# A two-block transformer kernel: four modulation chunks moved from TensorE to VectorE, one low part issued earlier, two orders on TensorE changed

## The reference, cut to what matters

```
# block 1, twice:
hn = rms_norm(x, ln1);  proj = hn @ w_in
y  = concat[ 6 MoBA heads, 4 mLSTM heads (normed, gated), 6 sliding-window heads with a sink ]
x  = x + y @ w_out
x  = x + square(relu(rms_norm(x, ln2) @ w_up)) @ w_down
# block 2, twice (with a second stream ctx of 256 tokens that shares weights):
mod   = silu(c) @ w_mod[l] + b_mod[l]          # 1024 -> 6*1024
mod_c = silu(c_ctx) @ w_mod[l] + b_mod[l]      # the same weights, for ctx
sh1, sc1, gt1, sh2, sc2, gt2 = split(mod, 6)
z = (rms_norm(x, g1) * (1 + sc1) + sh1) @ w_in_2   # attention over [x ; ctx], conv, Fourier
x = x + gt1 * merge(z);   x = x + gt2 * mlp(modulate(x, g2, sh2, sc2))
```

## Time and profile before

| | |
|---|---|
| median of 3 runs | 1736.59 us (1736.1 to 1736.89) |
| the profiled execution, its own time | 1736.67 us |
| its span in the trace | 1734.8 us |
| granted TensorE clock, mean over the span | 0.999 |
| RAW transfers of w_mod (1024 KB each) | 28 |
| WM transfers of w_mod (512 KB each) | 40 |
| DMA traffic | 343.67 MB, mean 198 GB/s |

### The profile page before, as it was taken

How to read it: one execution, slowest core, us unless ns; L and a number is a source line. 1 busy time by engine, 2 the same in 40 slices (tenths; PEclk the granted TensorE clock), 3 DMA queues, 4 the chain that set the end, 5 groups by cost and what they waited for, 6 DMA issues and landing times.

```text
span 1734.8 us, 23892 instructions
## 1 busy us (share of the span) xinstructions
PE 1715.5 (99%) x9753; PEld 1443.1 (83%) x9753; DVE 1246.3 (72%) x1518; ACT 930.4 (54%) x1238; POOL 46.7 (3%) x36
## 2 busy tenths in 40 slices
PE   8999999999999999999999999999999999999999
PEld 7868888886888898788888898778888887888887
DVE  6986888598687765577777857677666666775665
ACT  6555554556544554555555546546455546564453
POOL 0200000011000000000000000000000000000000
PEclk9999999999999999999999999999999999999999
DMA  8476776756777655455776554357555754345552
GB/s 297 157 245 204 243 243 209 264 157 219 257 239 238 203 190 173 146 174 190 265 236 226 183 170 168 112 192 244 196 193 194 235 176 147 134 146 194 194 194 73
DMA packets 226837, 343.67 MB, mean 198 GB/s; under 512 B 8109, under 2 KB 117033, under 8 KB 226729
## 3 DMA queue, kind: packets, MB, share of 16 engines
q1 hardware_dynamic: 225896, 340.87, 58.7%
q10 hardware_dynamic: 832, 1.28, 0.2%
HBM read 341.07 MB, written 1.06 MB: 197 GB/s over the span
## 4 chain that ended last, share of the span: by engine, by line
PE 90%; DVE 5%; ACT 1%; SPq 1%; issue 1%; DMA 1%; POOL 0%; POOLq 0%; ACTq 0%; DVEq 0%
PE PS L2263 15%; PE PS L2265 15%; PE PS L2264 15%; PE PS L2319 15%; PE PS L2323 8%; PE PS L2308 2%; PE PS L2309 2%; PE PS L2310 2%; PE PS L2706 1%; PE PS L2708 1%; PE PS L2707 1%; PE PS L2799 1%; PE PS L2787 1%; PE PS L2776 1%; PE PS L2726 1%
## 5 line engine op out<-in xcount | busy, mean ns | idle before, releaser
L1363 DVE TENSOR_TENSOR LO<-RAW,HI 128x2048 fp32r<-128x2048 f32 x271 | 618.6, 2290 | 263.7 <-ACT HI L795 262.9
L795 ACT CAST HI<-RAW 128x2048 fp32r<-128x2048 f32 (+1 forms) x273 | 518.9, 1905 | 191.2 <-PE PS L2265 99.7
L2319 PE MATMUL PS<-AHL,HI 128*128 128x512 f32 x1120 | 266.9, 390 | 0.0
L2263 PE MATMUL PS<-HI,HIDH 128*128 128x512 f32 x640 | 250.1, 391 | 0.0
L2264 PE MATMUL PS<-LO,HIDH 128*128 128x512 f32 x640 | 249.3, 389 | 0.0
L2265 PE MATMUL PS<-HI,HIDL 128*128 128x512 f32 x640 | 249.1, 389 | 0.0
L2319 PEld LDWEIGHTS PS<-AHL,HI 128*128 128x128 f32 x1120 | 206.7, 188 | 40.7
L2263 PE MATMUL PS<-HI,AHL 128*128 128x512 f32 (+2 forms) x640 | 232.2, 363 | 1.5 <-DVE AHL L1397 1.5
L2265 PE MATMUL PS<-HI,AHL 128*128 128x512 f32 (+2 forms) x640 | 227.3, 355 | 0.0
L2264 PE MATMUL PS<-LO,AHL 128*128 128x512 f32 (+2 forms) x640 | 227.2, 355 | 0.0
L795 ACT COPY U<-PS 128x512 f32<-128x512 f32 x70 | 41.1, 587 | 240.4 <-PE PS L2323 240.4
(11 more groups left out here) (364 smaller groups left out, 2311.2 us busy)
## 6 DMA issues: line engine op xcount, KB each, us to landing
RAW<-in_w_ff SPq DMA_DIRECT2D x96, 1024.0 KB, 5.3
RAW<-in_w_in SPq DMA_DIRECT2D x78, 1024.0 KB, 5.2
RAW<-in_w_up SPq DMA_DIRECT2D x32, 1024.0 KB, 7.0
RAW<-in_w_down SPq DMA_DIRECT2D x32, 1024.0 KB, 5.3
RAW<-in_w_mod SPq DMA_DIRECT2D x28, 1024.0 KB, 5.2
WM<-in_w_mod SPq DMA_DIRECT2D x40, 512.0 KB, 6.0
RAW<-in_w_o SPq DMA_DIRECT2D x12, 1024.0 KB, 5.1
RAW<-in_w_out SPq DMA_DIRECT2D x8, 1024.0 KB, 6.4
```

The lines of the kernel that those rows point to most:

```text
L795: return nc.scalar.copy(dst, src)
L1363: tt(LO[:, c % RAW_N, 0:n], RAW[:, c % RAW_N, 0:n], HI[:, NTH[c] % HL_N, 0:n].bitcast(F32), ALU.subtract).then_inc(s_lo, 1)
L2263: mm(o, th, hi[:, j, :], start=first and j == 0, stop=False)
L2319: mm(PS[:, b + q, :], hi[:, j, 128 * q:128 * q + 128], AHL[:, j, :, :].rearrange("p a n -> p (a n)"), start=j == 0, stop=False)
```

## The change

1. `OFF`, `group_of`, `SUMS`, `Half.sums`, `NSUM`: VectorE takes twelve groups instead of ten. `Layer.m_o` of layer 1 has two groups instead of four, so `modulation(4)` to `modulation(7)` are gone there (not in layer 0). The halves in feed-forward 1's second and third quarter are now for two streams instead of one, and feed-forward 3 has three groups instead of one. Which group is computed where moves accordingly, with the thresholds of the waits on `s_modc` and the sums' columns.
2. `norm_scales(0, 1)` on VectorE moves from the end of block 1 to pass 0, after `mod_sums`.
3. VectorE's `split(L.c_o)` moves ahead of the mLSTM's last two steps and of the sink, in both layers of block 1.
4. `four_banks`: two modulation chunks before the transposes and two behind, instead of three and one.
5. `scores2`: the 512 keys of x and ctx in two halves of 256, each with its own high, low-keys and low-queries products.

Cut to its core:

```
-OFF = (((10, (0, 1)), (11, (0, 1)), (12, (0, 1))), ((13, (0, 1)), (16, (0,)), (17, (0,))),
-       ((18, (0,)), (19, (0,)), (20, (0,))), ((21, (0,)),))
+OFF = (((8, (0, 1)), (9, (0, 1)), (10, (0, 1))), ((11, (0, 1)), (12, (0, 1)), (13, (0, 1))),
+       ((16, (0,)), (17, (0,)), (18, (0,))), ((19, (0,)), (20, (0,)), (21, (0,))))
...
-        self.m_o = Slot(self.c_in + 11, 4)
+        self.m_o = Slot(self.c_in + 11, 2 if l else 4)
...
 def modulation(j):
-    mod_chunk(L.m_o, j, 3)
+    if j < L.m_o.n:
+        mod_chunk(L.m_o, j, 3)
...
                 maxima(5)
+                split(L.c_o)
                 dve.wait_ge(s_rs, 5 * l + 4)
                 link(tt(hm, hm, RS...
                 tt(YN[...], HM[...], MN[...], ALU.mult).then_inc(s_src, 1)
                 tt(SKE[:, :, :], NB[:, 6:12, :], SK[...], ALU.add).then_inc(s_ske, 1)
-                split(L.c_o)
                 probabilities(5)
...
-            norm_scales(0, 1)
...
-                        mod_sums(0, 0, 0, ((0, 2, 40, 0), (2, 2, 40, 1)))
+                        mod_sums(0, 0, 0, ((0, 4, 32, 0), (4, 4, 32, 1)))
+                        norm_scales(0, 1)
...
             def four_banks(q):
-                for j in range(3):
+                for j in range(2):
                     mod_chunk(q.m_in, j, q.mod_bank)
...
-                mod_chunk(q.m_in, 3, q.mod_bank)
+                for j in range(2, 4):
+                    mod_chunk(q.m_in, j, q.mod_bank)
...
-                    for step in ("high", "low keys of x", "low keys of ctx", "low queries"):
+                    for half in range(n // S):
+                        for step in ("high", "low keys", "low queries"):
```

More of the change, by code:

```diff
@@ L65 @@
 M_SH, M_SC, M_GT = (0, 24), (8, 32), (16, 40)
-OFF = (((10, (0, 1)), (11, (0, 1)), (12, (0, 1))), ((13, (0, 1)), (16, (0,)), (17, (0,))),
-       ((18, (0,)), (19, (0,)), (20, (0,))), ((21, (0,)),))
+OFF = (((8, (0, 1)), (9, (0, 1)), (10, (0, 1))), ((11, (0, 1)), (12, (0, 1)), (13, (0, 1))),
+       ((16, (0,)), (17, (0,)), (18, (0,))), ((19, (0,)), (20, (0,)), (21, (0,))))
 WM_N, WM_LEAD = 3, 3
 def group_of(n):
-    return n if n < 10 else n + 4 if n < 12 else n + 10
+    return n if n < 8 else n + 6 if n < 10 else n + 12
 class Slot:
@@ L184, in sums @@
         g = self.group
-        return [g - 10 + 2 * s if g < 12 else g - 8 + 7 * s if g < 14 else g - 10 if g < 21 else 13 for s in self.streams]
+        return [g - 8 + 4 * s if g < 12 else g - 4 + 5 * s if g < 14 else g - 6 if g < 19 else g - 19 for s in self.streams]
 HALVES = []
@@ L192 @@
 HALF_AT = {(_h.mlp, _h.at): _h for _h in HALVES}
-NSUM = 14
-SUMS = (0, 8, 0, 4), (1, 36, 4, 13), (2, 40, 13, 14)
+NSUM = 15
+SUMS = (0, 16, 0, 8), (1, 36, 8, 15), (2, 48, 0, 3)
 NO_SLOT = Slot(0, 0)
@@ L1130, in gate_diagonals @@
                 act.wait_ge(s_modv, 1)
-                act.wait_ge(s_modc, 14 if q.layer else 10)
+                act.wait_ge(s_modc, 12 if q.layer else 8)
                 for k in range(8):
@@ L1543, in norm_scales @@
                     dve.wait_ge(s_modv, n + 2)
-                    dve.wait_ge(s_modc, 12)
+                    dve.wait_ge(s_modc, 10)
                 else:
-                    dve.wait_ge(s_modc, 4 + 6 * n)
+                    dve.wait_ge(s_modc, 4 + 4 * n)
+                    if n:
+                        dve.wait_ge(s_modv, 1)
                 w = 1 if l and n else 2
@@ L1597, in mlp @@
                         if i == 0 and j == 1 and q == PASSES[1].mlp:
-                            mod_sums(1, 1, 1, ((0, 2, 0, 0), (2, 5, 16, 0), (7, 2, 0, 1)))
+                            mod_sums(1, 1, 1, ((0, 2, 0, 0), (2, 3, 16, 0), (5, 2, 0, 1)))
             for t, (summed, mean) in enumerate(((s_ssf, s_msf), (s_ss, s_ms))):
@@ L2054, in _ @@
                     if k == 4 and q.p == 0:
-                        mod_sums(0, 0, 0, ((0, 2, 40, 0), (2, 2, 40, 1)))
+                        mod_sums(0, 0, 0, ((0, 4, 32, 0), (4, 4, 32, 1)))
+                        norm_scales(0, 1)
                     if k == 4 and q.mini:
-                        mod_sums(2, 0, 1, ((0, 1, 36, 0),))
+                        mod_sums(2, 0, 1, ((0, 3, 28, 0),))
                         norm_scales(1, 1)
@@ L2643, in _ @@
                 pe.wait_ge(s_oe, 6 * l + 6 + 1)
-                pe.wait_ge(s_modc, L.m_o.g + 4)
+                pe.wait_ge(s_modc, L.m_o.g + L.m_o.groups)
                 half_group(L.c_o + 2, 1, 0)
@@ L2760, in scores2 @@
                         pe.wait_ge(s_x2, q.att + v + 1)
-                    for step in ("high", "low keys of x", "low keys of ctx", "low queries"):
[L2762 to L2778, removed]
+                    for half in range(n // S):
+                        cols = slice(S * half, S * half + S)
+                        ctx = bool(q.stream) or half == 1
+                        for step in ("high", "low keys", "low queries"):
+                            for v in (v0, v0 + 1):
+                                h, t = head_tile(v)
+                                r = 64 * (h % 2)
+                                kv = 0 if h // 4 == h % 2 else 1
+                                low = step == "low queries"
+                                turned = (QTL if low else QT2)[r:r + 64, h // 2, 128 * t:128 * t + 128]
+                                if step == "low keys":
+                                    keys = (KLC if ctx else KLX)[r:r + 64, kv, :]
+                                else:
+                                    keys = KTB[r:r + 64, kv, S * ctx:S * ctx + S]
+                                last = mm(PS[:, 4 + v % 2, cols], turned, keys, start=step == "high", stop=low)
+                                if low and half == n // S - 1:
+                                    last.then_inc(s_s2, 1)
                 def turn2(v0):
```

## The result

The changed kernel takes 1740.32 us (median of 14 runs, 1738.31 to 1743.27), the kernel before 1736.59 us (14 runs, 1736.1 to 1739.28): ratio 1.0021, 95% interval 1.0014 to 1.0028. It is slower by 3.7 us, where 1.4 were forecast, and lies outside the range. One further run of the kernel before, beside the experiments e5 to e8, took 4396.66 us at full clock; its cause isn't known, and it is left out of every comparison.

A forecast was written before the change was run, and what follows sets the result against it. TensorE, busy 1715.5 of 1734.8 us, was taken as the bound. Terms 1.8 + 0 + 0 - 0.7 + 0.3 = +1.4 us on 1736.67 gave 1738.1, less 0.08: forecast 1738.0 us, range 1734.3 to 1739.8.

The forecast's parts named there:

- Low part ahead: End of block 1's heads: the earlier low part delays SKE, the bank's emptying and values(5), costing 0.9 us in each layer.
- Four chunks fewer: Block 1's second layer: removing four modulation chunks (4.0 us) gains 0; TensorE waits 2.3 us before values(5) instead.
- the standstill lowers TensorE's clock: Rival, 4%: the wait before values(5) drops TensorE to 1.2 GHz, doubling the 2.9 us output part behind it: 1741.0 us.
- VectorE's doubled halves: Feed-forward 1: 6.2 us more VectorE work in each of two quarters fits into idle time and slack, costing 0.
- Third opening: Third opening of the feed-forward: with two chunks ahead the transposes start earlier and the chain ends 0.7 us earlier.
- Scores: Attention scores in two halves: 0.91 us a pair instead of 0.90, +0.3 us over 16 pairs in two passes.
- The sum: Whole kernel: all terms together +1.4 us, forecast 1738.0 us, given 65%.
- third and fourth rival: Third, 7%: feed-forward 1's doubled VectorE halves make TensorE wait, 1742.0 us. Fourth, 4%: standstill lowers TensorE's clock, 1741.0.

The follow-up runs named there:

- e5: The kernel of e4 with the scores of the second layer's attention in their old order, whole rows of 512: 1736.47 us, ratio 1.0002.
- e8: The kernel before with only the third opening of the feed-forward in its new order, two chunks and two: 1736.39 us, ratio 0.9998.
- e2: The kernel before with only the low part moved ahead of the mLSTM's last steps and the sink, in both layers: 1738.39 us, ratio 1.0011.
- e1: The changed kernel with the low part put back behind the sink on VectorE, in both layers: 1738.62 us, ratio 1.0012.
- e3: The changed kernel with two unused products of 512 columns between the first output products and values(5), second layer only: 1738.63 us, ratio 1.0013.
- e6: The kernel of e5 with ready output products between the last heads' values and turns in layer 1, low parts moved to suit: 1735.32 us, ratio 0.9992.
- e4: The changed kernel with the sink's addition (SKE) ahead of the low part on VectorE: 1735.66 us, ratio 0.9996.

## Why the prediction was wrong

**Low part ahead: right.** +0.9 in each layer was forecast, by way of SKE, the sink's exponential and the bank's copy; the trace has 1.0 and 1.0, and e2 has 1.85 together. By its own rows the forecast should have said 0.8 (423.67 + 2.2 is 0.8 behind 425.06, and 114.36 + 2.2 is 0.8 behind 115.74); 0.1 of what it lacked is the dearer first product behind a standstill. ScalarE's idle 2.55 us for SKE stands in both layers, as was said.

**Four chunks fewer: right as work, wrong as a whole.** Their removal gave nothing (e1), and the standstill came: 2.11 us before values(5), forecast 2.3, and 0.56 ahead of the first output product.

**The failed step** is the rival *the standstill lowers TensorE's clock*, given 4%, so that the wait of 2.3 us entered the sum at nothing beyond itself. The fall is what the profiled run shows, and twelve of the fourteen runs have times that go with it. The reason against it was the earlier trace rows: a stretch of 4 us with 1.46 us of idle at full clock. That sum was of small pieces, and said nothing of 2.3 us in one piece; the prediction itself noted that no row showed one, and then weighed it as if it spoke against. The rival's price was off too, 2.9 us for the doubled output part: the lower level held for little over 3 us, where the doubled output part would have needed 5.8, and took 1.6 (the ledger) to 1.7 us (the stretches). The forecast 1738.0, 1.6 for the clock and the 0.5 us by which the other terms were larger make 1740.1, beside 1740.32 measured. e3 shows it by taking most of the standstill away and nothing else; e1 shows it with a standstill of another cause.

**VectorE's doubled halves: right.** VectorE is busy 25 us more, and TensorE's offset does not move in any feed-forward. (6.2 less the two idle times, 2.34 and 1.04, is 2.8 and not 2.9 us; nothing hangs on it.)

**Third opening: right, -0.6 for -0.7,** though the forecast's own rows give 0.5 for VectorE's first step (1361.71 - 1361.20) and nothing in them makes 0.7 of it. The gain is conditional, as e5 and e6 show: it falls to 0.05 or 0.15 where ScalarE can use the chunk of w_in 5.82 or 5.71 us after its issue instead of 5.14 (e4).

**Scores: +0.4 in the two passes in the ledger for +0.3.** The halves make up 0.2 of it (e4 against e5), 0.01 or 0.02 for each of 16 pairs. The pair's six rows in the changed kernel, the second pass, against the earlier trace rows:

```profile
1061.63 0.39 PE L2779 MATMUL PS<-KTB,QT 64*128 64x256 f32 x2
1061.85 0.28 PE L2779 MATMUL PS<-KLX,QT 64*128 64x256 f32 x2
...
1062.33 0.28 PE L2779 MATMUL PS<-KTB,QTL 64*128 64x256 f32 x2
```

The next product starts at 1062.54: 0.91 us, the number forecast, with 0.12 from step to step.

**The sum** was +1.4; the terms it had measure +1.9. Alone they would have been within the range. (The chances of the third and fourth rival add up to 11%, not 10%.) What else of the change makes 0.1 us in the second pass's scores and 0.1 in the third's stays open. So does where the clock falls in the few long runs of e3, e4 and e5 (7 of 33 lie over 1 us above their kernel's median, all at 0.998 or 0.997), since only one run of each was profiled. In e2, e6 and e8, where TensorE has chunks or products between the last heads, none of 33 does. That points to the thin stretch that the removed chunks left, without showing it: the kernel before has such runs too, if fewer (4 of 79, the two with a clock on record at 0.998).

## What to carry to other kernels

Work that fills a chain's waits is worth nothing when it is removed and something when it is replaced: e1 gained nothing, e6 1.15 us in the same place. Before an instruction is moved ahead on an engine, look for the shortest one that it passes and who waits for that; here 2.2 us put ahead of a 0.16 us addition held ScalarE, a bank and TensorE. And where TensorE is to stand still in one piece for longer than any piece in the profile, carry the lower clock behind it as a price with a real chance, not as a rarity: a row of a broken-up wait at full clock, such as the earlier trace rows, doesn't rule it out.

## What was not expected of the hardware

- A standstill of 1.97 us (e1) and one of 2.11 us (the changed kernel) were enough for the granted clock to fall to 0.50. The fall need not come within the standstill: in e1 the clock falls just ahead of the first product, but in the changed kernel values(5) starts at 427.15 at full pace, and the rows are stretched only from 428.2 on.
- With the same program the fall is there in some runs and not in others: one run of the changed kernel has a mean clock of 1.000, and the profiled one has the fall. Its runs spread over 5.0 us, e6's over 1.7. One fall explains 1.6 us of that spread; the rest is open.
- The same 1 MB transfer could be used 5.06 to 5.28 us after its issue in eight of the profiled runs and 5.71 and 5.82 us after it in e6 and e5. There the opening's gain of 0.6 us was nearly gone.
